# Expert weights in chunks of 2 MB, and gated rows added by products with diagonal matrices

## The chip, the cores and the metric

The kernel runs on one core of a Trainium2 chip. The core has TensorE (PE in the profile), VectorE (DVE), ScalarE (ACT), GpSimd (POOL) and a queue engine, SyncE (SP), beside 16 DMA engines that all queues share. The metric is the device time of one execution in microseconds (us), lower is better.

## What is computed

One layer: a token mixer, cross-attention, and a mixture of experts, then a last RMSNorm. There are 512 tokens of 1024 channels, all in f32. The change lies in the mixture of experts and in what follows it:

```python
logits = ht @ w_router + b_router
top_val, top_idx = lax.top_k(logits, 4)          # 4 of 32 experts for each token
gate = softmax(top_val)
# for each expert e and its tokens xb:
hc  = xb @ w1[e] + b1[e]                         # w1[e]: 1024 x 2048, 8 MB
glu, lin = min(hc[:, :1024], 7), clip(hc[:, 1024:], -7, 7)
act = glu * sigmoid(1.702 * glu) * (lin + 1)
y   = act @ w2[e] + b2[e]                        # w2[e]: 1024 x 1024, 4 MB
out[token] += gate * y                           # over the token's four experts
return rmsnorm(x + out, g_final)
```

All 32 experts are used, so 32 x 12 MB of expert weights are read from HBM.

## The kernel before

Each engine has a program written out by hand, in the order in which its instructions stand; semaphores order the engines among each other. A dense part comes first (token mixer, cross-attention, router), up to about 710 us. Then the experts run one by one.

**Chunks and ring.** An expert's weights come as 12 chunks of 1 MB: 8 of layer one (`W1`), a row of 2048 numbers (8 KB) in each of 128 partitions, and 4 of layer two (`W2`), two rows of 1024 beside each other in a partition, 8 KB too. `EC` is 12. The ring has `SLOTS` = 15 places: 12 in the tile `ring` and 3 in `moe`, the last of which lies over the f32 biases. SP issues all loads (`load`, L485). For the first 15 it waits until the dense part has freed the memory (L488 to L497): two go at 596 us, two until 617, two at 665, and nine at 710. From then on `refill` loads chunk k when PE has used chunk k - 15, which PE tells by `w_used`, once a chunk. A chunk has landed when all its 16 DMA engines have reported to `w_ring` of its place.

**PE.** For each expert `up` (L1902) adds into PSUM, chunk by chunk: for each chunk, group j of 32 tokens (an expert takes 3, 3 or 2 groups in turn) and quarter s of the columns, one product of 128 x 32 by 128 x 512. Four of them with different s run beside each other in the array. An f32 product shows as two records. `down` (L1926) does the same with layer two and 256 columns. The order is up(p), turns of small tiles, down(p-1). `x_turn` (L1860) transposes an expert's tokens, and a set of 32 products at L1979 makes the first expert's. The last expert's layer two is `last_down` (L1952), whose result stays on the chip (`y_last`).

**The end.** Results of experts go to HBM (`y_main`, the last but one expert's to `y_late`). POOL gathers them by token with indirect DMAs, 512 KB each: 16 `early_row` (L656), u = 4t + k for token tile t and choice k, into eight places `y_rows`, and four `late_row` (L661). The first waits until the last chunk of down(30) has landed. In DVE's `add_row` (L1510) and `add_late` (L1516) each is multiplied by its gate and added to `res`. PE's `last_rows` (L1970) makes the last expert's share, four token tiles of two 64-row products each, and DVE's `add_last` (L1544) adds it. ACT sums squares (L1037), then DVE and ACT make the norm (L1549, L1551, L1040, L1555) and SP stores the tile (L539). POOL, DVE and PE first read `n_over`, a count of experts with more tokens than fit; the trace shows no such work.

**The last chunk** is loaded in two pieces (L524), 8 partitions with a semaphore of their own (`w_edge`) and 120 partitions.

## Time and profile before

| | us |
|---|---|
| median of 3 runs | 1824.0 |
| lowest, highest | 1822.47, 1825.4 |
| the profiled execution | 1821.48 |
| its span in the profile | 1819.8 |

The mean granted clock of TensorE in it was 0.987 of full speed. Busy in the span: PE 1700.5 us, DVE 459.2, ACT 385.8, POOL 101.3. The 16 DMA engines moved 505.72 MB, a mean of 278 GB/s.

A profile is of one execution. "DMA share" is the mean busy share of the 16 DMA engines; packets whose times overlap make it a little more than 1. Windows give a stretch in us from the span's start. A row in order of time has its start, its length, the engine and line, the operation, and in square brackets the idle time ahead of it with what ended it. SPq is the instruction queue of SP, and its DMA_DIRECT2D rows are issues, not transfers.

### The profile page before, as it was taken

What the parts mean: (1) busy time and instruction counts of PE and PEld (TensorE: products, weight loads), DVE (VectorE), ACT (ScalarE), POOL (GpSimd) and SP (SyncE); (2) the same over time, 40 slices, a digit from 0 to 9 for tenths busy, and PEclk for the clock granted to TensorE, in tenths of its full rate; (3) what the DMA queues carried; (4) which work ended last, traced back from release to release, by engine and by line L of the source; (5) the groups of instructions that cost most, each with busy time, mean ns of one, the idle gap of its engine ahead of it and who ended that gap; (6) DMA issues with size and microseconds to landing.
All of it is one profiled execution on the core that took longest, in us unless ns stands there. A gap on an engine that the chain in (4) does not pass through costs nothing.

```text
span 1819.8 us, 36146 instructions
## 1 busy us (share of the span) xinstructions
PE 1700.5 (93%) x15618; PEld 943.4 (52%) x15618; DVE 459.2 (25%) x846; ACT 385.8 (21%) x602; POOL 101.3 (6%) x185
## 2 busy tenths in 40 slices
PE   7999999999999997999999999999999999999982
PEld 5766687788788766434343434333343343343330
DVE  4354426324544345700010101010000000000007
ACT  5464233324334325001000000000000010000001
POOL 0010000000000020000000000000000000000012
PEclk9999999999999999999999999999999999999996
DMA  7202221224225333999999999999999999999996
GB/s 237 70 24 82 82 101 50 70 93 162 93 84 194 116 93 148 363 392 376 410 399 407 402 407 401 403 410 398 410 404 402 411 404 402 411 401 409 409 333 256
DMA packets 105718, 505.72 MB, mean 278 GB/s; under 512 B 10519, under 2 KB 21287, under 8 KB 56327
## 3 DMA queue, kind: packets, MB, share of 16 engines
q1 hardware_dynamic: 83911, 461.40, 64.5%
q0 software_dynamic: 8352, 29.01, 5.1%
q10 hardware_dynamic: 13312, 13.12, 2.1%
q8 instruction: 125, 2.05, 0.5%
q14 instruction: 18, 0.15, 0.0%
HBM read 488.28 MB, written 15.20 MB: 277 GB/s over the span
## 4 chain that ended last, share of the span: by engine, by line
PE 59%; SPq 18%; DMA 13%; DVE 4%; issue 2%; ACT 2%; POOL 1%; ACTq 0%; DVEq 0%
SPq L485 18%; PE ps L1902 16%; PE ps L1582 9%; PE ps L1583 9%; PE ps L1584 9%; PE ps L1926 7%; DMA ring<-in_w_exp_in 5%; DMA ring<-in_w_exp_out 5%; DMA moe<-in_w_exp_in 2%; PE ps L1679 1%; PE ps L1734 1%; PE ps L1753 1%; DVE work L1510 1%; DMA work<-y_main,work 1%; PE ps L467 1%
## 5 line engine op out<-in xcount | busy, mean ns | idle before, releaser
L1902 PE MATMUL ps<-ring,moe 128*32 128x512 f32 x4408 | 490.2, 594 | 24.0 <-DMA ring<-in_w_exp_in 23.6
L1902 PEld LDWEIGHTS ps<-ring,moe 128*32 128x32 f32 x4408 | 131.2, 110 | 366.2 <-issue 270.4
L1477 DVE TENSOR_SCALAR moe<-ps 128x768 f32<-128x768 f32 (+1 forms) x32 | 28.0, 875 | 883.6 <-PE ps L1902 883.6
L1926 PE MATMUL ps<-ring,moe 128*32 128x256 f32 x4320 | 240.4, 379 | 7.4 <-DMA ring<-in_w_exp_out 7.4
L1051 DVE TENSOR_TENSOR wl<-raw,wh 128x1024 fp32r<-128x1024 f32 x104 | 126.3, 1224 | 259.4 <-ACT wh L712 259.4
L1926 PEld LDWEIGHTS ps<-ring,moe 128*32 128x32 f32 x4320 | 129.3, 110 | 108.5 <-DMA ring<-in_w_exp_out 12.6
L712 ACT ACTIVATE wh<-raw 128x1024 fp32r<-128x1024 f32 x104 | 108.9, 1057 | 255.8 <-PE ps L1584 255.2
L1582 PE MATMUL ps<-oph,wh 128*128 128x512 f32 x384 | 151.5, 394 | 2.4 <-DVE work L1184 1.6
L952 ACT ACTIVATE moe<-ps 128x768 f32<-128x768 f32 (+1 forms) x32 | 23.8, 744 | 596.5 <-DVE moe L1477 596.5
L1583 PE MATMUL ps<-opl,wh 128*128 128x512 f32 x384 | 150.2, 391 | 0.0
L1584 PE MATMUL ps<-oph,wl 128*128 128x512 f32 x384 | 150.1, 391 | 0.0
L1902 PE MATMUL ps<-moe 128*32 128x512 f32 x1096 | 124.4, 594 | 7.4 <-DMA moe<-in_w_exp_in 7.3
L1582 PE MATMUL ps<-wh,oph 128*128 128x512 f32 x288 | 113.8, 395 | 3.8 <-DVE opl L1222 3.0
L1583 PE MATMUL ps<-wl,oph 128*128 128x512 f32 x288 | 112.2, 389 | 0.0
L1584 PE MATMUL ps<-wh,opl 128*128 128x512 f32 x288 | 112.1, 389 | 0.0
L1582 PEld LDWEIGHTS ps<-oph,wh 128*128 128x128 f32 x384 | 72.8, 190 | 19.4 <-issue 3.6
L1902 PEld LDWEIGHTS ps<-moe 128*32 128x32 f32 x1096 | 32.4, 110 | 93.2 <-issue 64.7
L1584 PEld LDWEIGHTS ps<-oph,wl 128*128 128x128 f32 x384 | 72.5, 189 | 15.5
L1583 PEld LDWEIGHTS ps<-opl,wh 128*128 128x128 f32 x384 | 72.6, 189 | 14.5
L612 POOL CAST sel_c<-work 96x32 bf16 (+1 forms) x64 | 16.8, 288 | 933.8 <-DVE moe L1331 905.3
L1582 PEld LDWEIGHTS ps<-wh,oph 128*128 128x128 f32 x288 | 54.1, 188 | 17.4 <-issue 4.7
L1584 PEld LDWEIGHTS ps<-wh,opl 128*128 128x128 f32 x288 | 54.1, 188 | 11.5
(298 smaller groups left out, 1520.1 us busy)
## 6 DMA issues: line engine op xcount, KB each, us to landing
ring<-in_w_exp_in SPq DMA_DIRECT2D x205, 1024.0 KB, 28.6
ring<-in_w_exp_out SPq DMA_DIRECT2D x103, 1024.0 KB, 28.8
moe<-in_w_exp_in SPq DMA_DIRECT2D x51, 1024.0 KB, 29.1
raw<-in_w_in SPq DMA_DIRECT2D x26, 1024.0 KB, 5.2
moe<-in_w_exp_out SPq DMA_DIRECT2D x24, 1024.0 KB, 28.3
raw<-in_w_ckv SPq DMA_DIRECT2D x8, 1024.0 KB, 5.1
y_main<-moe ACTq DMA_DIRECT2D x84, 96.0 KB, 9.3
raw<-in_w_ret_o SPq DMA_DIRECT2D x4, 1024.0 KB, 5.1
```

What stands on the lines that cost most here:

```text
L467: ins = nc.tensor.matmul(ps[:, 6 + dt, :], v_x[:, m, a:a + P], prob_t[:, hd % 2, m * T:(m + 1) * T], start=(m == 0), stop=(m == MT - 1))
L485: sp.dma_start(held(s), expert_chunk(e, c)).then_inc(w_ring[s], 16)
L712: nc.scalar.activation(wh[:, slot, :], raw[:, c % RAW, g % 2 * PC:(g % 2 + 1) * PC], ACT.Copy).then_inc(w_hi, 1)
L952: nc.scalar.activation(glu_s[:, 0:g], ps[:, 0:g, 0:256].rearrange("p j (n a) -> p j a n", a=2), ACT.Silu, scale=ALPHA).then_inc(s_ready, 1)
L1051: nc.vector.tensor_tensor(wl[:, slot, :], raw[:, g // 2 % RAW, g % 2 * PC:(g % 2 + 1) * PC], wh[:, slot, :], ALU.subtract).then_inc(w_lo, 1)
L1477: nc.vector.tensor_scalar(act_n[:, 0:g], ps[:, 0:g, 256:512].rearrange("p j (n a) -> p j a n", a=2), 1.0 - LIMIT, 1.0 + LIMIT, ALU.max, AL ...
L1510: nc.vector.scalar_tensor_tensor(res[:, t, :], y_rows[u % ROWS], gate[:, t, k:k + 1], res[:, t, :], ALU.mult, ALU.add).then_inc(row_used, 1)
L1582: nc.tensor.matmul(o, a_hi_, b_hi_, start=start, stop=False)
L1583: nc.tensor.matmul(o, a_hi_, b_lo_, start=False, stop=False)
L1584: return nc.tensor.matmul(o, a_lo_, b_hi_, start=False, stop=stop)
L1902: ins = nc.tensor.matmul(ps[32 * s:32 * s + 32, j, :], xt[:, k, 32 * j:32 * j + 32], w[:, s, :, :], start=False, stop=(k == KT - 1), tile_ ...
L1926: ins = nc.tensor.matmul(y_bank(s, j), at[:, a, j, q, :], w[:, a, s, :], start=False, stop=(q == W2 - 1 and a == 1), tile_position=(0, 32 ...
```

## The change

Chunks become 2 MB: a partition holds two rows of layer one or four of layer two, 16 KB in one piece of HBM. `W1` is 4, `W2` 2, `EC` 6. The ring has 7 places, six in `ring` and one, number 5 (`EDGE`), in `moe`; `w_used` counts once for 2 MB. SP fills three places before the dense part ends and four after it.

As partition p of chunk c now holds rows 2p and 2p+1 of its 256 rows, the tokens' transposes take every other channel (`by_pair`). For layer two a partition holds rows 4p to 4p+3, so `up` takes the columns of each product in pairs: two numbers, then two left out. The products stay the same in number and size.

The last chunk is loaded in eight pieces of 2, 4, 6, 8, 10, 12, 14 and 72 partitions.

At the end DVE first makes eight matrices of 128 x 128, a gate on the diagonal (`gate_d`, in memory of the router). PE multiplies with them the four late gathers and the four early ones of the last token tile, and adds them in PSUM to the last expert's share. DVE's `add_row` 12 to 15 and all `add_late` are gone. The late gathers have other places in memory.

```diff
-W1 = KT
-W2 = KT // 2
+W1 = KT // 2
+W2 = KT // 4
 EC = W1 + W2
-SLOTS = EC + 3
+EH = 2 * CH
+SLOTS = EC + 1
...
-        ring = sb("ring", [P, EC, CH])
+        ring = sb("ring", [P, EC, EH])
...
         def held(s):
-            return ring[:, s, :] if s < EC else m_(5120 + CH * (s - EC), CH)
+            return m_(5120, EH) if s == EDGE else ring[:, s if s < EDGE else s - 1, :]
...
-        late = ring[:, 9:11, :].rearrange("p c (b n) -> p (c b) n", b=2)
+        late = [m_(6144, D), m_(9216, D), m_(10240, D), w_(4096, D)]
...
             if c < W1:
-                return w_exp_in[0, bass.ds(e, 1), c * P:(c + 1) * P, :].rearrange("o p n -> p (o n)")
+                return w_exp_in[0, bass.ds(e, 1), 2 * P * c:2 * P * c + 2 * P, :].rearrange("o (p a) n -> p (o a n)", a=2)
             q = c - W1
-            return w_exp_out[0, bass.ds(e, 1), 2 * P * q:2 * P * q + 2 * P, :].rearrange("o (p a) n -> p (o a n)", a=2)
+            return w_exp_out[0, bass.ds(e, 1), 4 * P * q:4 * P * q + 4 * P, :].rearrange("o (p a) n -> p (o a n)", a=4)
...
-                elif 2 <= s < 6:
-                    sp.wait_ge(w_lo, 2 * (DENSE - RAW + s - 1))
-                elif s == 6:
+                elif 1 <= s < 3:
+                    sp.wait_ge(w_lo, 2 * (DENSE - RAW + 2 * s))
+                elif s == 3:
                     sp.wait_ge(w_used, DP)
-                elif s == EC + 1:
+                elif s == EDGE:
...
-            for rows, landed in ((slice(0, 8), w_edge), (slice(8, P), w_ring[(CHUNKS - 1) % SLOTS])):
+            row = 0
+            for n, landed in zip((2, 4, 6, 8, 10, 12, 14), w_edge):
+                rows = slice(row, row + n)
                 sp.dma_start(held((CHUNKS - 1) % SLOTS)[rows, :], expert_chunk(final, EC - 1)[rows, :]).then_inc(landed, 16)
+                row += n
...
-            def add_late(t):
-                dve.wait_ge(late_in[t], 16)
-                dve.wait_ge(row_used, 4 * t + 4)
-                nc.vector.scalar_tensor_tensor(res[:, t, :], late[:, t, :], names["glate"][:, t:t + 1], res[:, t, :],
-                                               ALU.mult, ALU.add).then_inc(late_used, 1)
+            def diagonal(n, column):
+                nc.vector.tensor_scalar(gate_d[n], ident, column, None, ALU.mult).then_inc(diag_ready, 1)
...
+            def by_pair(rows, k):
+                return rows.rearrange("p (c n a) -> p c a n", c=W1, a=2)[:, k // 2, k % 2, :]
...
-                for k in range(KT):
-                    w = chunk_in(None if over is not None else up_chunk(n, k), over, k).rearrange("p (g s n) -> p s g n", g=2, s=4)
-                    for j in range(g):
-                        for s in range(4):
-                            ins = nc.tensor.matmul(ps[32 * s:32 * s + 32, j, :], xt[:, k, 32 * j:32 * j + 32], w[:, s, :, :],
+                for c in range(W1):
+                    w = chunk_in(None if over is not None else up_chunk(n, c), over, c).rearrange(
+                        "p (a g u n l v) -> p a u l g n v", a=2, g=2, u=2, l=2, v=2)
+                    for a in range(2):
+                        k = 2 * c + a
+                        for j in range(g):
+                            for s in range(4):
+                                ins = nc.tensor.matmul(ps[32 * s:32 * s + 32, j, :], xt[:, k, 32 * j:32 * j + 32], w[:, a, s // 2, s % 2, :, :, :],
...
+            def gated_rows(t, n, rows, stop=False):
+                for h in range(2):
+                    ins = nc.tensor.matmul(ps[:, 2 * t + h, :], gate_d[n], rows[:, 512 * h:512 * h + 512],
+                                           start=False, stop=stop, skip_group_check=True)
+                return ins
+
             def last_rows():
                 pe.wait_ge(gl_kept, 1)
                 pe.wait_ge(y_kept, NE)
                 for t in range(TT):
+                    own_rows(t)
+                pe.wait_ge(diag_ready, TT + TOPK)
+                for t in range(TT - 1):
+                    pe.wait_ge(late_in[t], 16)
+                    gated_rows(t, t, late[t], stop=True).then_inc(last_done, 1)
+                for k in range(TOPK):
+                    u = (TT - 1) * TOPK + k
+                    pe.wait_ge(row_in[u % ROWS], 16 * (u // ROWS + 1))
+                    gated_rows(TT - 1, TT + k, y_rows[u % ROWS])
+                pe.wait_ge(late_in[TT - 1], 16)
+                gated_rows(TT - 1, TT - 1, late[TT - 1], stop=True).then_inc(last_done, 1)
```

SP's queue at the end of the weights, before: the last whole chunk, the two pieces of the last one, and the load of `n_over` that follows.

```order
L485 DMA ring<-in_w_exp_out 128x2048
L524 ISA [waits w_used]
L524 DMA ring<-in_w_exp_out 8x2048
L524 ISA
L524 DMA ring<-in_w_exp_out 120x2048
L527 TENSOR_LOAD work [waits route_done]
```

And now (rows that only count registers left out):

```order
L489 DMA ring<-in_w_exp_out 128x4096
L535 ISA [waits w_used]
L535 DMA ring<-in_w_exp_out 2x4096
...
L535 DMA ring<-in_w_exp_out 4x4096
...
L535 DMA ring<-in_w_exp_out 6x4096
...
L535 DMA ring<-in_w_exp_out 8x4096
...
L535 DMA ring<-in_w_exp_out 10x4096
...
L535 DMA ring<-in_w_exp_out 12x4096
...
L535 DMA ring<-in_w_exp_out 14x4096
...
L538 DMA ring<-in_w_exp_out 72x4096
L541 TENSOR_LOAD work [waits route_done]
```

Two issues of the last chunk have become eight; nothing else has come between.

PE's queue from the last chunk on, before; the last two rows are `last_rows`.

```order
L1952 MATMUL ps<-ring,moe 32x512 [waits w_ring8,w_edge]
L1952 MATMUL ps<-ring,moe 32x512 x7
L2013 TENSOR_LOAD work [waits route_done]
...
L2016 UNCONDITIONAL_BRANCH [waits y_kept]
...
L1970 MATMUL ps<-moe 128x512 [waits y_kept,gl_kept]
L1970 MATMUL ps<-moe 128x512 x7
```

And now:

```order
L1967 MATMUL ps<-ring,moe 32x512 [waits w_edge4,w_edge5,w_edge3,w_edge6,w_edge2,w_ring2,w_edge1,w_edge0]
L1967 MATMUL ps<-ring,moe 32x512 x15
L2046 TENSOR_LOAD work [waits route_done]
...
L2049 UNCONDITIONAL_BRANCH [waits y_kept]
...
L1982 MATMUL ps<-moe 128x512 [waits y_kept,gl_kept]
L1982 MATMUL ps<-moe 128x512 x7
L1987 MATMUL ps<-moe,work 128x512 [waits late_in0,diag_ready]
...
L1987 MATMUL ps<-moe,work 128x512 [waits late_in1]
...
L1987 MATMUL ps<-moe,work 128x512 [waits late_in2]
...
L1987 MATMUL ps<-work 128x512 [waits row_in4]
...
L1987 MATMUL ps<-work 128x512 [waits row_in5]
...
L1987 MATMUL ps<-work 128x512 [waits late_in3]
```

Behind the last expert's share stand sixteen full products with the diagonal matrices, each pair behind the gather that it needs; the rows of the other gathers are left out.

DVE's queue at the very end, before, from the norm of the first tile on.

```order
L1551 RECIPROCAL small<-small 128x1 [waits dve_chain]
L1510 SCALAR_TENSOR_TENSOR work<-work 128x1024 [waits row_in4]
L1555 SCALAR_TENSOR_TENSOR work<-work,small 128x1024 [waits n_sqrt]
...
L1510 SCALAR_TENSOR_TENSOR work<-work 128x1024 [waits row_used,row_in5]
...
L1510 SCALAR_TENSOR_TENSOR work<-moe,work 128x1024 [waits row_used,row_in6]
...
L1516 SCALAR_TENSOR_TENSOR work<-ring,work 128x1024 [waits row_used,late_in3]
L1544 TENSOR_TENSOR work<-ps,work 128x1024 [waits late_used,last_done]
L1549 TENSOR_SCALAR small<-small 128x1 [waits n_sq]
...
L1555 SCALAR_TENSOR_TENSOR work<-work,small 128x1024 [waits n_sqrt]
```

And now:

```order
L1564 RECIPROCAL small<-small 128x1 [waits dve_chain]
L1568 SCALAR_TENSOR_TENSOR work<-work,small 128x1024 [waits n_sqrt]
L1562 TENSOR_SCALAR small<-small 128x1 [waits n_sq]
...
L1568 SCALAR_TENSOR_TENSOR work<-work,small 128x1024 [waits n_sqrt]
L1557 TENSOR_TENSOR work<-ps,work 128x1024 [waits last_done]
L1562 TENSOR_SCALAR small<-small 128x1 [waits n_sq]
...
L1568 SCALAR_TENSOR_TENSOR work<-work,small 128x1024 [waits n_sqrt]
```

The four `add_row` and the `add_late` of the last tile are gone from between the norms, so the last `add_last` stands right behind the third norm, with only PE to wait for.

## Rows read from the trace of the kernel before

**Rows 1.** The page, part 2: DMA engines, busy tenths in 40 slices of the span.

```profile
DMA  7202221224225333999999999999999999999996
```

**Rows 2.** Busy time by stretch (start:end us, length, engines, PEclk, DMA share, GB/s).

```profile
core 0: us, PE busy (x) PEld busy (x) DVE busy (x) ACT busy (x) POOL busy (x), PEclk, DMA share, GB/s
740.00:800.00 60.00, 58.06 (x652) 21.86 (x648) 29.90 (x83) 5.52 (x8) 2.78 (x6) 0.97 0.94 358
1200.00:1300.00 100.00, 94.41 (x1172) 36.84 (x1168) 6.95 (x12) 8.67 (x14) 4.44 (x9) 1.00 1.02 406
1750.00:1765.00 15.00, 12.52 (x200) 6.14 (x196) 1.38 (x2) 1.09 (x2) 0.74 (x1) 1.00 0.69 220
```

**Rows 3.** PE in order of time, a wait for a chunk (start, length).

```profile
1149.91 1.92 PE L1902 MATMUL ps<-ring,moe 128*32 128x512 f32 x16 [0.91 <-DMA ring<-in_w_exp_in]
```

**Rows 4.** The page, part 6: a DMA issue, KB each, median us to landing.

```profile
ring<-in_w_exp_in SPq DMA_DIRECT2D x205, 1024.0 KB, 28.6
```

**Rows 5.** DMA queues from 800 to 1700 us: packets, MB, share of 16 engines.

```profile
q1 hardware_dynamic: 46975, 342.09, 94.0%
...
q10 hardware_dynamic: 11520, 9.97, 3.2%
```

**Rows 6.** The same for 1412 to 1430 us, in which only weights move.

```profile
q1 hardware_dynamic: 1035, 7.54, 101.2%
```

**Rows 7.** The chain that ended last, three experts (start, length, what).

```profile
922.68 20.60 PE ps L1902 x192
...
956.56 13.74 PE ps L1902 x128
...
1014.14 20.60 PE ps L1902 x192
```

**Rows 8.** SP queue in order of time: the loads that fill the ring.

```profile
664.94 47.86 SPq L485 DMA_DIRECT2D ring<-in_w_exp_in  x8
712.84 1.47 SPq L485 DMA_DIRECT2D moe<-in_w_exp_in  x3
738.68 0.33 SPq L485 DMA_DIRECT2D ring<-in_w_exp_in  x1
741.25 8.05 SPq L485 DMA_DIRECT2D ring<-in_w_exp_out  x4
```

**Rows 9.** PE in order of time, the first two experts.

```profile
735.86 20.77 PE L1902 MATMUL ps<-ring,moe 128*32 128x512 f32 x192
...
761.81 11.48 PE L1902 MATMUL ps<-ring,moe 128*32 128x512 f32 x96
```

**Rows 10.** The end, all engines in order of time.

```profile
1764.26 0.99 POOL L656 DMA_INDIRECT work<-y_main,work  x1 [40.85 <-DMA ring<-in_w_exp_out]
...
1779.75 2.48 PE L1952 MATMUL ps<-ring,moe 128*32 128x512 f32 x16 [3.75 <-DMA ring<-in_w_exp_out]
...
1787.01 5.78 PE L1970 MATMUL ps<-moe 64*128 64x512 f32 x16 [4.79 <-issue]
...
1795.42 0.93 POOL L661 DMA_INDIRECT ring<-y_late,work  x1 [0.30 <-issue]
...
1810.91 1.28 DVE L1516 SCALAR_TENSOR_TENSOR work<-ring,work 128x1024 f32<-128x1024 f32 x1
1812.30 1.23 DVE L1544 TENSOR_TENSOR work<-ps,work 128x1024 f32<-128x1024 f32 x1
...
1815.37 1.28 DVE L1555 SCALAR_TENSOR_TENSOR work<-work,small 128x1024 f32<-128x1024 f32 x1 [0.27 <-ACT small L1040]
```

**Rows 11.** DMA issues of the whole run: the gathers of late rows.

```profile
ring<-y_late,work POOLq DMA_INDIRECT x4, 7.7
```

**Rows 12.** The chain that ended last: eight records, four full f32 products.

```profile
658.37 3.71 PE ps L467 x8
```

**Rows 13.** Busy time by stretch at the end, columns as in rows 2.

```profile
1785.00:1790.00 5.00, 2.99 (x8) 1.56 (x10) 4.79 (x4) 0.00 (x0) 3.84 (x4) 0.50 0.97 357
1790.00:1795.00 5.00, 2.79 (x10) 0.84 (x8) 4.69 (x5) 0.00 (x0) 4.03 (x4) 0.88 1.01 359
```

More of the change, by code:

```diff
@@ L518, in _ @@
                         refill(some[i], W1 + q, down_chunk(1 + i, q), m * (TURN * EC))
-            final = expert_at(NE - 1)
+            *some, final = [expert_at(NE - 3 + i) for i in range(3)]
+            for i in range(2):
+                for c in range(W1):
+                    refill((some[1], final)[i], c, up_chunk(NE - 2 + i, c))
+                for q in range(W2):
+                    refill(some[i], W1 + q, down_chunk(NE - 3 + i, q))
             for q in range(W2 - 1):
@@ L534, in _ @@
                         for c in range(EC):
-                            load(b % NE, c, c)
+                            load(b % NE, c, c if c < EDGE else c + 1)
             for tt in range(TT):
@@ L1962, in gates_turn, with own_rows @@
                 ins.then_inc(gl_made, 1)
+            def own_rows(t):
+                for h in range(2):
+                    rows = slice(64 * h, 64 * h + 64)
+                    nc.tensor.matmul(ps[:, 2 * t + h, :], gate_l[rows, t * P:(t + 1) * P], y_last[rows, :],
+                                     start=True, stop=False, skip_group_check=True)
+            def gated_rows(t, n, rows, stop=False):
+                for h in range(2):
+                    ins = nc.tensor.matmul(ps[:, 2 * t + h, :], gate_d[n], rows[:, 512 * h:512 * h + 512],
+                                           start=False, stop=stop, skip_group_check=True)
+                return ins
             def last_rows():
```

71 lines of the change are left out of this document (35 added, 36 removed).

## The prediction

> **What bounds the kernel now.** I read the page's slices first, then windows, queues and the order of time at both ends. From about 720 us to 1765 us the DMA engines are full [rows 1], and in the middle of the expert phase their share is 1.02 while PE is busy 94% of the time [rows 2]: PE works off a chunk of 16 records in 1.92 us and then waits 0.9 us for the next one [rows 3]. The arithmetic agrees. In 900 us the weight queue moves 342.09 MB [rows 5], so an expert of 12.58 MB takes 12.58 / 342.09 x 900 = 33.1 us. PE, when it had chunks in stock, made three experts between 922.68 and 1014.14, 30.5 us each [rows 7]. So the transfer of the weights is the bound, by 2.6 us an expert. A chunk lands 28.6 us after its issue [rows 4], though one is issued every 33.1 / 12 = 2.8 us: some ten are on their way at once, and no wait of SP is on the path.
>
> Two stretches are different. Between 740 and 800 us the DMA share is only 0.94 [rows 2]: there the ring is full of landed chunks and SP waits for PE. And between 1750 and 1765 us, with chunks still missing, the share is 0.69 at 220 GB/s [rows 2]: some of the 16 engines have finished their part of the last chunks and others have not. The last chunk starts PE at 1779.75 [rows 10]. Behind it DVE is the bound: of the end at 1816.65 the last steps are the late row of the last tile at 1810.91, the last addition at 1812.30, and the norm [rows 10].
>
> **Packets of 16 KB.** A packet has a part that does not depend on its size. Weights alone: 1035 packets and 7.54 MB take 101.2% of 16 engines for 18 us, 291.5 us of engine time [rows 6]. ACT's stores have small packets: 11520 and 9.97 MB take 3.2% of 16 x 900 us, 460.8 us [rows 5]. Two equations, a for a packet and b for a MB: 1035a + 7.54b = 291.5 and 11520a + 9.97b = 460.8 give a = 7.4 ns and b = 37.6 us. With the weight row of rows 5 for the other one a is 6.5 ns, and the rounding of 3.2% is worth 0.7 ns: 5.8 to 8.1 ns. A chunk counts 144 packets (46975 for 342.09 MB [rows 5]: 128 of data, and 16 which report). Six of the 384 chunks are loaded in the dense part; for the other 378 half of 54,432 packets go. The gain is 27,216 x 7.4 ns / 16 = 12.6 us (9.9 to 13.8). No row here has a weight packet of 16 KB, so nothing shows that a piece of that size travels whole and without a price of its own; the lower bound is no gain, and below it a loss of the same size. I take 12.6, since the rows from 1 KB to 8 KB lie on one line. An expert then takes 32.7 us, and PE's 30.5 still hide behind that.
>
> The Trainium skill's page "DMA: Bandwidth & Descriptors", in the section on the anatomy of one DMA, gives a transfer 2.0 us of fixed cost beside its bytes. For 189 transfers fewer that would be an estimate of 378 us, if they stood one behind the other. Rows 4 speak against it here: the cost lies beside some ten other transfers. I leave 2% to it.
>
> **Places of 2 MB.** The ring falls from 15 MB to 14, and SP gets a place back only when PE has used 2 MB. Just before PE's even MB the queue is 1 + 1 = 2 MB behind where it was. This costs only while the ring is what limits, 740 to 800 us. The fill after the dense part is nine chunks in one go at 710 to 714 us [rows 8] and becomes eight; the first refills, at 738.68 and 741.25 [rows 8], become one at 741.2. PE's first expert takes 20.77 us for 8 MB and the second starts at 761.81 [rows 9]; the first refill of the second comes when 2 MB are used, 5.2 us later, instead of 2.6. At the 0.38 to 0.42 MB/us of the stream 2 MB are 4.8 to 5.3 us, and a little is lost on top while it catches up: I take +5.5. Bounds: 1 MB, 2.6, and 3 MB, 8. After 800 us PE gains on the DMA and the places are plentiful: beside the 2 MB in PE's hands 12 MB are on their way or landed, 33 us of stream against the 28.6 us that a chunk needs in the queue.
>
> **Strided operands.** `up` now reads two numbers and skips two, and the transposes take every second channel. No row of before has a product of this kind. They are the same products; if they ran slower, the 2.2 us an expert between 30.5 and 32.7 are the cover. `up` is (20.60 + 13.74 + 20.60) / 3 = 18.3 us of an expert [rows 7], so the cover is gone from 12% on. I take nothing.
>
> The Trainium skill's "SBUF — State Buffer", in its section on the DMA port swizzle, states that a read runs at full bandwidth with at least two hits in each line of 16 bytes. Two f32 out of four are just two hits. By it this edit costs nothing, and no run here shows it.
>
> **The last chunk.** Eight issues stand where two stood, but issued some 30 us ahead of need, like the ones before them [rows 4]; their time at SP is hidden, and SP has nothing behind them but the outputs. The split moves rows between DMA engines, towards those that a small piece uses. Whether these are the ones that are early, rows 2 do not say. A whole engine's share of 2 MB is 8 packets of 16 KB, 8 x 0.62 = 5 us; that is the most it can gain, if the late engines get none. If a late one gets more than its share I give it 3 us. Between them I take 0. One more term: from the landing of the chunk that lets POOL go (1764.26) to the last one (1779.75) 4 MB take 15.5 us [rows 10], where at 0.42 MB/us they would take 10; the row gathers take the rest, packet by packet. With half as many weight packets among them I take 1.5 us off.
>
> So PE gets its last chunk 12.6 - 5.5 + 1.5 = 8.6 us earlier, at 1771.2 (without the start of the stream moved, since the loads at 710 us hang on the dense part alone).
>
> **The tail.** Before, from 1779.75: 2.48 us of work, 4.8 us until `last_rows` start at 1787.01, 5.78 us of them, and DVE behind [rows 10]. Now the chunk is 32 records, 3.8 us [rows 3] to 5.0; I take 4.4. Then 4.8, and 5.8 for the last expert's share. Then 16 full f32 products: four take 3.71 us [rows 12], one 0.93, together 14.8. Then the last `add_last` and the norm, 1812.30 to 1816.65, 4.35 us, and 0.1 to hand over. The end is 1771.2 + 4.4 + 4.8 + 5.8 + 14.8 + 4.5 = 1805.5, against 1816.65: -11.2. Two other ways must be shorter. The gathers: the last one was issued at 1795.42 and takes 7.7 us [rows 10, 11], 1803.1; now 7.1 earlier, 1796.0; two products and the norm behind it end at 1802.4. DVE: sixteen row additions and four late ones become twelve, it saves 8 x 1.28 [rows 10] = 10.2 us of a chain that was full, and ends its first three tiles before PE is ready with the last. The eight diagonals are small and stand where DVE waits for the first gather. So PE takes DVE's place as the bound, and most of what DVE saves goes into the 14.8 us of PE.
>
> **Sum.** On the profiled execution's 1821.5 us: -12.6 + 5.5 - 1.5 - 2.6 = -11.2, 1810.3. The median of the runs is 2.5 us above it, so I forecast 1824.0 - 11.2 = 1813. Its own range, from the bounds of packet, ring and last chunk: 1805 to 1820.
>
> **Rivals.**
> (1) The 16 KB packets are no cheaper, say because they travel in pieces. Then 12.6 us are missing: 1825, no change. For it: no row has such packets. Against it: the law holds over a factor of eight.
> (2) PE is cold at the end. It stands idle before `last_rows`, and the granted clock there is 0.50, then 0.88 after some us of work [rows 13]. At 1.2 GHz the 16 products take twice 14.8 us: 1828, slower. It decides from about 12 of the 16 products in the low clock. Against it: PE now works without a stop, and the clock rose during the 5.78 us before.
> (3) Strided reads hold PE up. From 12% on in `up` PE is the bound; at twice the time an expert takes 30.5 + 18.3 = 48.8 us, 16 more than 32.7, for 31 experts 500 us: some 2310 us, far slower.
> (4) The coarse ring lets DMA queues run dry later on too, because a chunk must land on all engines, the late ones too, before its place comes back. At 1 us an expert 1839. Against it: 33 us of stock.
> (5) Better than the sum: the split spares the late engines (5 us), or the ring costs only its 1 MB (3 us): 1803.
>
> **Chances.** The forecast 0.60; (1) 0.11; (2) 0.07; (3) 0.07; (4) 0.05; (5) with the 2% above 0.10. A measurement of this kernel tells 0.2% from no change, 3.6 us. Faster is the forecast and (5), 0.70; within 0.2% is (1) and a little of the forecast's upper end, 0.13; slower is (2), (3), (4) and the loss below (1), 0.17. The range takes in (1), (2) and most of (5): 1803 to 1829, leaving out (3), (4) and the rest of (5).
>
> **What would show it.** Right: half as many packets in the weight queue, and less than 33.1 us an expert in mid phase, with MB in 900 us up by 1.2% to about 346; a lower DMA share than 0.94 in 740 to 800; `up` at 20.6 us where PE has stock; the last chunk at about 1771; PE busy without a gap to the last product, at about 1801, and DVE waiting for it. Wrong: a weight queue with as many packets or the same MB in 900 us; a longer `up`; a PE clock of 0.5 in the last products; DVE or a gather named as what the last addition waits for.

## The result, and the profile after

The changed kernel takes 1837.7 us (median of 6 runs, 1833.8 to 1841.6). The kernel before took 1824.9 (6 runs beside it, 1822.5 to 1825.8). The ratio is 1.0074, interval 1.0061 to 1.0088: 13.5 us slower (12.8 by the medians), where 11 us less were forecast. Two of the four runs of experiment 8 below came out in a slower state (2141.4 and 2149.5 us) and are left out. The profiled execution took 1835.6 us with a span of 1833.9, against 1821.5 and 1819.8.

Busy time by stretch of the changed kernel (start:end us, length, busy us of PE, PEld, DVE, ACT, POOL with counts, PEclk, DMA share, GB/s), as rows 2:

```profile
740.00:800.00 60.00, 58.48 (x625) 23.65 (x616) 31.49 (x93) 4.06 (x6) 3.82 (x7) 0.97 0.87 321
800.00:900.00 100.00, 100.00 (x1229) 43.69 (x1231) 6.95 (x12) 9.57 (x17) 4.47 (x9) 1.00 1.00 379
1750.00:1765.00 15.00, 10.96 (x104) 3.28 (x96) 3.08 (x10) 1.09 (x2) 0.00 (x0) 1.00 0.98 294
1765.00:1780.00 15.00, 11.53 (x153) 5.75 (x153) 0.00 (x0) 0.00 (x0) 3.79 (x4) 0.77 0.74 200
1780.00:1800.00 20.00, 13.99 (x97) 4.90 (x99) 3.25 (x3) 1.47 (x3) 5.55 (x6) 0.75 0.94 237
```

Two stretches went wrong. From 740 to 900 us the stream is slower than before: 321 GB/s to 800 us, where rows 2 had 358. And at the end the rate falls to 294, 200 and 237 GB/s, and stays there to 1800 us. In the first and third of these stretches the DMA engines are nonetheless busy (0.98, 0.94): the packets themselves take longer. Between them, from 1765 to 1780 us, a part of the engines is idle as well (0.74).

The DMA queues from 800 to 1700 us (packets, MB, share of 16 engines), as rows 5:

```profile
q1 hardware_dynamic: 23575, 343.35, 93.7%
q0 software_dynamic: 2736, 9.44, 3.3%
q10 hardware_dynamic: 11520, 9.97, 3.2%
```

Half the packets, as forecast, for 343.35 MB instead of 342.09: 0.4% more, not 1.2%.

The chain that ended last, three experts (start, length, what), as rows 7:

```profile
900.68 21.74 PE ps L1916 x183
922.42 1.13 PE ps L1871 x8
...
956.52 10.36 PE ps L1940 x192
...
968.25 14.47 PE ps L1916 x118
...
996.36 21.74 PE ps L1916 x183
```

A three-group `up` (L1916) takes 21.74 us instead of 20.60, a two-group one 14.47 instead of 13.74, the transposes of `x_turn` (L1871) 1.13. Three experts, 900.68 to 996.36, take 95.7 us where they took 91.5. `down` (L1940, 10.36) has its time of before: its operands are read as before.

PE in order of time at the end, as rows 10:

```profile
1791.29 3.61 PE L1967 MATMUL ps<-ring,moe 128*32 128x512 f32 x32
1797.05 5.25 PE L1967 MATMUL ps<-ring,moe 128*32 128x512 f32 x32 [2.15 <-DMA ring<-in_w_exp_out]
1806.86 5.40 PE L1982 MATMUL ps<-moe 64*128 64x512 f32 x16 [4.57 <-issue]
1812.43 5.39 PE L1987 MATMUL ps<-moe,work 128*128 128x512 f32 x12 [0.16 <-DMA moe<-y_late,work]
...
1824.52 1.88 PE L1987 MATMUL ps<-work 128*128 128x512 f32 x4
```

The last chunk starts PE at 1797.05. Before that was at 1779.75, and 1771.2 was forecast. From there on the forecast holds nearly: 5.25 us for the chunk (4.4 forecast), 4.57 idle (4.8), 5.40 for `last_rows` (5.8), then PE almost without a gap through the products with diagonal matrices. The way from the last chunk to the end (1830.8) is 33.7 us; 36.9 before, 34.3 by the terms of the forecast.

The last chunk isn't alone in being late. The chain that ended last goes through the row gathers, of which these are two pieces (start, length, what):

```profile
1777.77 21.53 DMA work<-y_main,work
...
1804.53 7.76 DMA moe<-y_late,work
```

One gather of 512 KB takes 21.53 us from its issue to its landing. The first late row lands at 1812.29, when PE is just through with the last expert's share (1812.26). So the way through the late chunk and the way through the slow gathers are equally long.

So of 14.1 us of span, 17.3 arise before the last chunk starts PE, and 3.2 come back in the tail. The experiments take the 17.3 apart.

### The profile page after: what moved, and what is told of

Its sections match the earlier page's. It is cut to its first block, busy times and chain, and to the rows that moved or that the text cites. A ratio compares the mean times of both kernels' runs of the same rounds, so it can differ in the third digit from the quotient of the medians.

```text
span 1833.9 us, 35462 instructions
## 1 busy us (share of the span) xinstructions
PE 1757.5 (96%) x15650; PEld 998.6 (54%) x15650; DVE 451.4 (25%) x846; ACT 386.0 (21%) x602; POOL 101.5 (6%) x185
## 4 chain that ended last, share of the span: by engine, by line
PE 79%; DMA 15%; DVE 3%; ACT 2%; issue 1%; SPq 0%; POOL 0%; ACTq 0%; POOLq 0%; DVEq 0%
PE ps L1916 28%; PE ps L1940 12%; DMA ring<-in_w_exp_in 10%; PE ps L1590 9%; PE ps L1591 9%; PE ps L1592 9%; DMA ring<-in_w_exp_out 2%; PE ps L1871 1%; PE ps L1687 1%; DMA work<-y_main,work 1%; PE ps L1742 1%; PE ps L1761 1%; PE ps L1904 1%; PE ps L1880 1%; PE ps L471 1%; PE ps L1987 1%
## 5 line engine op out<-in xcount | busy, mean ns | idle before, releaser
L1916 PE MATMUL ps<-ring,moe 128*32 128x512 f32 x4688 | 542.2, 616 | 8.6 <-DMA ring<-in_w_exp_in 8.2
L1916 PEld LDWEIGHTS ps<-ring,moe 128*32 128x32 f32 x4688 | 166.8, 108 | 365.8 <-issue 335.3
L1940 PE MATMUL ps<-ring,moe 128*32 128x256 f32 x4704 | 266.5, 383 | 9.8 <-DMA ring<-in_w_exp_out 6.2
L1940 PEld LDWEIGHTS ps<-ring,moe 128*32 128x32 f32 x4704 | 143.6, 111 | 121.7 <-issue 9.7
L1916 PE MATMUL ps<-moe 128*32 128x512 f32 x816 | 96.4, 615 | 0.9 <-DMA moe<-in_w_exp_in 0.9
L1916 PEld LDWEIGHTS ps<-moe 128*32 128x32 f32 x816 | 30.5, 108 | 61.5 <-issue 58.1
```

The costliest lines, as they stand in the source:

```text
L1916: ins = nc.tensor.matmul(ps[32 * s:32 * s + 32, j, :], xt[:, k, 32 * j:32 * j + 32], w[:, a, s // 2, s % 2, :, :, :], start=False, stop=(k ...
L1940: ins = nc.tensor.matmul(y_bank(s, j), at[:, a % 2, j, 2 * q + a // 2, :], w[:, a, s, :], start=False, stop=(q == W2 - 1 and a == 3), tile ...
```

## Experiments

Times are compared with the kernel before run on the same chip beside each: its medians were 1825.6, 1825.0 and 1823.2 us for the three groups of four kernels (experiments 1 to 4, 5 to 8, 9 to 12). Where two experiments are compared, differences of medians are given, and of the ratios where they say something else. One ratio is known to about 2 us, a difference of two to some 3 us. "Best" is the kernel of experiment 5.

**1. The last chunk in one transfer** (changed kernel):

```
-            for n, landed in zip((2, 4, 6, 8, 10, 12, 14), w_edge):
-                rows = slice(row, row + n)
-                sp.dma_start(held((CHUNKS - 1) % SLOTS)[rows, :], expert_chunk(final, EC - 1)[rows, :]).then_inc(landed, 16)
...
+            load(final, EC - 1, (CHUNKS - 1) % SLOTS)
```

> The changed kernel, but the last weight chunk comes in one transfer of 128 partitions instead of eight transfers of 2 to 72 partitions. Theory A: transfers of a few partitions put the 16 DMA engines in each other's way, so that the whole stream runs at about half rate (200 to 237 GB/s between 1765 and 1800 us, packets of 16 KB at 1.0 to 1.2 us instead of 0.62) while they are in flight; without them the rate stays near 400 GB/s up to the last packet, the last chunk starts PE some 8 to 12 us earlier than 1797, and the time is about 1827 (1824 to 1831). Rival B: the low rate at the end is that of the engines that are late anyhow (half the engines have finished), and the split spares the late ones; then the last chunk comes 0 to 5 us later and the time is 1838 to 1843.

Measured: 1821.0 us, ratio 0.9979 (0.9968 to 0.9990). The eight transfers alone cost the changed kernel 17 us (by the two intervals some 14 to 20): more than its whole loss. Its busy time by stretch, and PE at the end in order of time:

```profile
1750.00:1765.00 15.00, 13.67 (x120) 3.69 (x116) 0.00 (x0) 0.81 (x1) 0.00 (x0) 1.00 0.99 414
1765.00:1780.00 15.00, 13.31 (x201) 6.38 (x193) 3.09 (x10) 1.09 (x2) 5.58 (x6) 1.00 0.69 273
1780.00:1800.00 20.00, 16.09 (x100) 4.69 (x102) 15.12 (x12) 3.35 (x5) 10.39 (x11) 0.74 0.87 323
```

```profile
1787.51 9.23 PE L1958 MATMUL ps<-ring,moe 128*32 128x512 f32 x64
1798.51 3.70 PE L1973 MATMUL ps<-moe 64*128 64x512 f32 x16 [1.77 <-issue]
```

To 1765 us the stream runs at 414 GB/s, where the changed kernel had 294. The chunk is no longer waited for: PE runs through the last four MB, 64 records from 1787.51, in one piece. The gathers are faster too. From 1780 to 1795 us the row of their queue is, for the changed kernel and for this one:

```profile
q0 software_dynamic: 773, 2.82, 83.5%
```

```profile
q0 software_dynamic: 1346, 4.90, 86.1%
```

773 packets in 83.5% of 16 engines' 15 us are 0.26 us each, 1346 in 86.1% are 0.15. So the cut slowed the other queue's packets as well.

In this execution PE itself is what is late. Not by strided reads: `down` of expert 30, which reads as before, takes 17.7 us (1767.66 to 1785.4) where experiment 12 has 10.6. The last 24 of its 192 records alone take 6.8 us, with stops of 0.4 to 0.8 us between them, for which the profile names no cause. The changed kernel's trace and those of experiments 2 and 3 have such stops too, Best's and experiment 12's have none. The profiled execution took 1825.5 us and is the slowest of the ten, so a part of these stops isn't in the median of 1821.0.

The time is below the 1824 to 1831 of theory A, in its direction; rival B is out.

**2 to 4. The tail alone, the plain reads, and the cut of the kernel before.** Experiment 2 puts the diagonal matrices into the kernel before, as the changed kernel has them:

```
-            def add_late(t):
...
+            def diagonal(n, column):
+                nc.vector.tensor_scalar(gate_d[n], ident, column, None, ALU.mult).then_inc(diag_ready, 1)
...
-            add_row(12)
...
-            add_late(3)
```

Experiment 3 reads layer one with contiguous columns in the changed kernel (and so its biases, and the channels of the transposes; as many numbers are multiplied, but not the reference's):

```
-    "p (a g u n l v) -> p a u l g n v", a=2, g=2, u=2, l=2, v=2)
+    "p (a g s n) -> p a s g n", a=2, g=2, s=4)
```

Experiment 4 loads the last chunk of the kernel before in one transfer:

```
-            for rows, landed in ((slice(0, 8), w_edge), (slice(8, P), w_ring[(CHUNKS - 1) % SLOTS])):
-                sp.dma_start(held((CHUNKS - 1) % SLOTS)[rows, :], expert_chunk(final, EC - 1)[rows, :]).then_inc(landed, 16)
+            load(final, EC - 1, (CHUNKS - 1) % SLOTS)
```

> The kernel before with one part of the change alone: late rows and last tile by products with diagonal gate matrices; weights as before, in chunks of 1 MB. Theory: the way from the start of PE's last chunk to the end falls from 36.9 us to about 34, as it did in the changed kernel (33.7), and the time is 1822 (1820 to 1824). Rival: the f32 products at the end are in PE's low clock when the last chunk is smaller, or the tail of the changed kernel is only shorter since its last chunk comes so late that all row gathers are long done; then the tail is 36 to 42 us here and the time 1824 to 1830.

> The changed kernel with the operands of layer one read as contiguous columns and the transposes taking contiguous channels: the same number of products and bytes, but channels are paired with the wrong rows and columns of the weights, so layer one's numbers are not the reference's. Theory A: the strided f32 reads are what makes a group of `up` take 21.8 us instead of 20.6; with plain columns `up` is 20.6 again and x_turn 0.8, three experts take 91.5 us instead of 95.7, and the ring gives places back sooner between 740 and 900 us: of the 9 us lost there about 3 to 4 come back, time 1834 (1832 to 1836). Rival B: `up` is slow for another reason (the write of a packet of 16 KB into a partition that PE reads); then it stays at 21.8 us and the time at 1838. Rival C: `up` is fast again but the stream is the bound all the same and the time moves by less than 1 us.

> The kernel before, but its last chunk in one transfer of 128 partitions instead of 8 and 120. Theory A (transfers of fewer than 128 partitions slow the stream while they are in flight; before, 1751 to 1757 at about 230 GB/s): the last chunk comes 2 to 4 us earlier, time 1822 (1820 to 1823). Rival B (the split moves work from late to early engines and is worth its price): 1825 to 1830.

Measured: 1821.6 us for the tail alone (ratio 0.9977, 0.9966 to 0.9988); 1833.6 for plain columns (1.0039, 1.0027 to 1.0052), 4.1 under the changed kernel by the medians and 6 by the ratios; 1822.4 for the kernel before with its last chunk whole (0.9986, 0.9973 to 0.9998). In all three the first theory holds; in experiment 4 the interval just leaves out no change. In experiment 3 a three-group `up` takes 20.60 us and an `x_turn` 0.81.

What the cut of 8 and 120 does to a packet can be read from the weight queue in 1751 to 1757 us, before and in experiment 4:

```profile
q1 hardware_dynamic: 182, 1.26, 89.0%
```

```profile
q1 hardware_dynamic: 278, 1.99, 80.0%
```

With the cut 182 packets take 89.0% of 16 engines' 6 us, 0.47 us each; without it 278 take 80.0%, 0.28 us each.

**5. Both good edits on chunks of 1 MB**: the diagonal matrices and the last chunk whole, in the kernel before (the diffs of experiments 2 and 4 together).

> The kernel before (chunks of 1 MB) with the products with diagonal matrices and the last chunk in one transfer of 128 partitions. Each alone gave 4.0 and 3.2 us. Theory A: they act at different places (the arrival of the last chunk, the way behind it) and add up: time 1818 (1816.5 to 1820). Rival B: with the chunk earlier the row gathers are what is late at the end, and the second gain is lost: 1820 to 1823. Beside it the changed kernel with its last chunk whole (1821.0) says what chunks of 2 MB are worth by themselves: by A they cost 3 us, by B nothing.

Measured: 1814.1 us, ratio 0.9941 (0.9928 to 0.9955), 10.9 us under the kernel before and the fastest of all. That is more than the 7.2 us of the two alone, which neither theory gave. One reading is that each edit makes way for the other: with the products at the end the chain of row additions on DVE is no longer what is late [rows 10], so an earlier chunk, and earlier gathers, are worth their whole time. That is argued and not shown: in the traces of experiments 2 and 4 ACT stands idle for 20.43 and 17.74 us ahead of its work on the results of expert 30, in the end for something that the profile does not name, and PE, which follows, runs through the last four MB in one piece there too. The chain of work at the end of Best:

```profile
1767.53 11.65 DMA work<-y_main,work
...
1779.20 1.30 DVE work L1510
...
1784.53 7.64 DMA moe<-y_late,work
...
1792.30 13.99 PE ps L1965 x32
1806.31 1.24 DVE work L1544
...
1809.37 1.28 DVE work L1555
```

Here the last chunk isn't in the chain, and DVE only with one addition, which gives a gather its place. The row gathers are: the first late row lands at 1792.17 (7.64 us after its issue), and 14 us of products and the norm follow. PE waits only 0.87 us for that row, so the way through the last chunk is nearly as long. Against Best, the changed kernel with its last chunk whole is 7 us slower. So chunks of 2 MB, with the strided reads that they bring, are a loss.

**6. Two transfers of 1 MB for each chunk of 2 MB** (changed kernel, last chunk whole):

```
-                sp.dma_start(held(s), expert_chunk(e, c)).then_inc(w_ring[s], 16)
+                for h in range(2):
+                    sp.dma_start(held(s)[:, CH * h:CH * h + CH], expert_chunk(e, c)[:, CH * h:CH * h + CH]).then_inc(w_ring[s], 16)
...
-                    pe.wait_ge(w_ring[k % SLOTS], 16 * (k // SLOTS + 1))
+                    pe.wait_ge(w_ring[k % SLOTS], 32 * (k // SLOTS + 1))
```

> The changed kernel with its last chunk whole, and each 2 MB chunk loaded by two transfers of 1 MB, the first and the second half of every row: packets of 8 KB as before, places of the ring, strided reads and tail as changed. It takes the packet size alone away. Theory A: the packet's own share of 7.4 ns is real and hidden only in part behind PE, whose expert takes 31.9 us: where the stream is the bound (after 1350 us) it is worth 0.36 us an expert over some 13 experts, 5 us: time 1826 (1824 to 1833). Rival B: packets of 16 KB are no cheaper than two of 8 KB, or PE hides them wholly: the time stays at 1821.

Measured: 1822.9 us, ratio 0.9994 (0.9985 to 1.0003), against 0.9979 with whole packets. The difference, 1.9 us by the medians and 2.7 by the ratios, lies between the theories, and the intervals overlap: packets of 16 KB, together with half as many transfers, are worth 0 to 5 us here, and surely not 12.6.

**7. The last chunk in eight transfers of 128 partitions** (changed kernel; an eighth of the columns each):

```
-            for n, landed in zip((2, 4, 6, 8, 10, 12, 14), w_edge):
...
+            w = EH // 8
+            for n, landed in enumerate(w_edge + [w_ring[(CHUNKS - 1) % SLOTS]]):
+                sp.dma_start(held((CHUNKS - 1) % SLOTS)[:, w * n:w * n + w],
+                             expert_chunk(final, EC - 1)[:, w * n:w * n + w]).then_inc(landed, 16)
```

> The changed kernel with its last chunk in eight transfers, as there, but each of all 128 partitions and an eighth of the columns (packets of 2 KB), instead of 2 to 72 partitions. Theory A: what slows the stream is that a transfer covers only some of the partitions, so that the engines write through the same few ports of SBUF; with 128 partitions in each the time is that of the whole transfer, 1821 (1820 to 1824, some 1 us for 7/8 more packets and 7 more issues). Rival B: it is the number of transfers (eight completions, eight waits); then the time stays at 1836 to 1838.

Measured: 1825.2 us, ratio 0.9999 (0.9989 to 1.0009). Twelve of the 17 us are back with as many transfers and as many waits as in the changed kernel. The stream keeps its rate for the most part: in the three stretches of the end it moves 373, 303 and 363 GB/s, where the changed kernel moved 294, 200 and 237 and experiment 1 moved 414, 273 and 323. The last of them:

```profile
1780.00:1800.00 20.00, 7.09 (x34) 1.90 (x36) 13.01 (x11) 1.88 (x2) 15.84 (x12) 0.65 0.98 363
```

Eight transfers with their packets of 2 KB cost some 4 us, a little above what theory A gave (the two aren't taken apart); the partitions in each cost the rest.

**8 and 9. The same cut far from the end.** In 28 experts the first chunk of layer two comes in two transfers, of 64 and 64 partitions (experiment 8) or 8 and 120 (experiment 9):

```
+   for rows, landed in ((slice(0, 64), w_mid[i]), (slice(64, P), w_ring[k % SLOTS])):
+       sp.dma_start(held(k % SLOTS)[rows, :], expert_chunk(some[i], W1)[rows, :]).then_inc(landed, 16)
```

> The changed kernel with its last chunk whole, and in 28 of the 32 experts the first chunk of layer two in two transfers of 64 partitions each, on the same queue, instead of one of 128. It measures the price of a transfer of few partitions far from the end, where nothing else changes. Theory A: half of the partitions reach half of the ports, so each such chunk goes at half rate and takes some 5 us more: with 28 of them, up to 140 us, of which PE hides at most 1 us an expert: time 1920 to 1965, packets of 16 KB at twice 0.61 us while they are in flight. The Trainium skill's page "SBUF — State Buffer", section on the DMA port swizzle, says that partitions 0 to 63 cover only the 8 even ports; its rule would be seen here in this way. Rival B: only counts of partitions that 16 does not divide, which leave engines out, are dear (2 to 14, 72, 120); 64 is divisible, and the time stays at 1821 to 1825.

> The changed kernel with its last chunk whole, and in 28 experts the first chunk of layer two in transfers of 8 and 120 partitions instead of one of 128, as the kernel before cuts its last chunk. 64 + 64 at this place cost 300 us, 10.7 us a chunk. Theory A: only transfers that leave half of the ports out are dear; 120 partitions reach all of them, and the price is that of 8 partitions, under 1 us a chunk: 1825 to 1850. Rival B: any transfer which isn't of 128 partitions hands its rows to the engines in another order, so that several write through one port at a time; then the price is that of the kernel before, where this cut of 1 MB cost 3.2 us, for 2 MB 3 to 10 us a chunk: 1900 to 2100.

Measured: 2101.6 us (two runs, 2096.7 and 2106.4) and 2150.9 us (four runs, ratio 1.1772, 1.1737 to 1.1806). Against 1821.0 that is 281 and 330 us, for 28 chunks 10.0 and 11.8 us each. (The 10.7 us in the expectation of experiment 9 were worked out from a median of 2123.9.) Experiment 8, by stretch: a stretch with whole chunks, and one with a cut chunk in flight; below them the weight queue in the same two stretches.

```profile
1012.00:1020.00 8.00, 8.00 (x97) 3.36 (x90) 0.00 (x0) 1.47 (x3) 0.00 (x0) 1.00 1.00 423
1022.00:1040.00 18.00, 14.24 (x113) 4.32 (x108) 0.00 (x0) 0.00 (x0) 0.00 (x0) 0.91 1.02 230
```

```profile
q1 hardware_dynamic: 227, 3.33, 98.1%
```

```profile
q1 hardware_dynamic: 281, 3.88, 94.1%
```

The engines are full in both (1.00 and 1.02), but move 423 GB/s in the one and 230 in the other. By the queue's row 227 packets take 98.1% of 16 engines for 8 us, 0.55 us each with the small ones among them; later 281 take 94.1% for 18 us, 0.96 us each. Experiment 9:

```profile
1121.00:1147.00 26.00, 16.54 (x146) 4.91 (x138) 0.00 (x0) 1.68 (x3) 0.00 (x0) 0.87 1.02 225
1148.00:1154.00 6.00, 2.46 (x12) 0.58 (x16) 0.00 (x0) 0.00 (x0) 0.00 (x0) 0.55 1.02 405
```

225 GB/s for 26 us around a cut chunk, 405 behind it. The changed kernel's stream is much like this from 1755 to about 1805 us: 180 to 256 GB/s in steps of 5 us, though with a part of the engines idle in some. Theory A of experiment 9 (only transfers which leave half of the partitions out are dear) is refuted; a cut of 8 and 120 is at least as dear as one of 64 and 64. Both expectations were too small as well: 2 MB at half rate would be 5 us more, and the cut costs 10 to 12. The slow stretch takes in the chunks around it.

The Trainium skill's "DMA: Bandwidth & Descriptors", in its sections on a DMA's semaphore count and on the descriptor swizzle, says that a transfer of 128 partitions gives each engine rows of one SBUF port, and that other counts are dealt over the largest k up to 16 that divides them (8 engines for 8 rows, 15 for 120, 12 for the changed kernel's 72). The measured halving fits engines that then meet at the same ports; no row here shows a port, so that stays an inference. The Trainium skill's "SBUF — State Buffer", section on the DMA port swizzle, makes 64 partitions reach half of the ports, which gives the half rate of experiment 8 but not its length.

**10. The grain of the ring alone**, in Best: two chunks of 1 MB are asked for when both places of 14 are free.

```
-                sp.wait_ge(w_used, turn + (DP + k - SLOTS + 1))
+                sp.wait_ge(w_used, turn + (DP + (k | 1) - 13))
```

**11. The strided reads alone**, in Best (the biases too; the numbers of layer one are not the reference's):

```
-    w = chunk_in(...).rearrange("p (g s n) -> p s g n", g=2, s=4)
+    w = chunk_in(...).rearrange("p (g u n l v) -> p u l g n v", g=2, u=2, l=2, v=2)
...
-    xrows[:, k * P:(k + 1) * P]
+    xrows.rearrange("p (c n a) -> p c a n", c=KT // 2, a=2)[:, k // 2, k % 2, :]
```

**12. Chunks of 2 MB without strided reads**: the changed kernel with the diffs of experiments 1 and 3 (again not the reference's numbers).

> The best kernel so far (before, with diagonal products and the last chunk whole; chunks of 1 MB, 1814.1) with waits of the ring that make it as coarse as the changed kernel's: two chunks of 1 MB are asked for together, when both their places of 14 are free, the fifteenth place unused but at the start. Packets, reads and products as before. It takes the grain of the ring alone. Theory A: it costs what the prediction took for it, 5.5 us (the ring is what limits from 740 to 900 us): 1819.5 (1817 to 1822), DMA share in 740 to 800 us down from 0.93 to about 0.87. Rival B: a start that comes later is made good later, since PE has stock: 1814 to 1816.

> The same best kernel with chunks of 1 MB, but layer one's weights and biases read as two numbers of every four, and the channels taken by the transposes as every second one, as in the changed kernel; the numbers multiplied are not those of the reference in layer one. It takes the strided reads alone. Theory A: a group of `up` takes 21.8 us instead of 20.6 here too, three experts 95.7 instead of 91.5, and though the stream's 33.1 us an expert cover this in the middle, the time grows by about 4 us, as the changed kernel lost 4.1 with plain columns: 1818 (1816.5 to 1820); PE busy 100% from 800 to about 1350 us. Rival B: with places of 1 MB the ring covers it and nothing is lost: 1813 to 1815.5. Rival C: the reads are slow only beside packets of 16 KB; `up` stays at 20.6.

> The changed kernel with its last chunk whole and plain columns and channels in layer one (which numbers are multiplied there is not the reference's): chunks of 2 MB, ring of 14 MB, packets of 16 KB, no strided reads. It closes the square of reads and chunk sizes. Theory A: the three terms add up: against the best kernel +5.5 for the ring, -2.6 for the packets (two transfers of 1 MB gave 1822.9 against 1821.0), time 1817 (1815 to 1819). Rival B: without strided reads PE no longer hides the cheaper packets, and they give up to 12.6 us from 800 us on: 1808 to 1812.

Measured, with Best at 1814.1 us (0.9941): the grain 1819.6 (0.9986, 0.9975 to 0.9997), 5.5 us more by the medians and 8 by the ratios; the strided reads 1817.9 (0.9975, 0.9955 to 0.9995), 3.8 and 6 us; 2 MB with plain reads 1815.5 (0.9958, 0.9944 to 0.9973), 1.4 and 3 us, which the intervals do not tell from nothing. All three times are those of theory A. Best by stretch, then the first stretch of experiments 10 and 12, and three of 11:

```profile
740.00:800.00 60.00, 58.11 (x652) 21.87 (x648) 32.47 (x93) 4.71 (x7) 2.78 (x6) 0.97 0.93 355
800.00:900.00 100.00, 100.00 (x1272) 40.24 (x1268) 6.95 (x12) 9.76 (x16) 4.48 (x9) 1.00 1.01 396
900.00:1350.00 450.00, 438.92 (x5428) 171.80 (x5420) 32.87 (x56) 40.58 (x65) 20.64 (x42) 1.00 1.02 404
```

```profile
740.00:800.00 60.00, 58.06 (x652) 21.84 (x648) 29.69 (x82) 5.52 (x8) 2.78 (x6) 0.97 0.89 342
```

```profile
740.00:800.00 60.00, 58.06 (x652) 22.08 (x644) 32.85 (x94) 4.71 (x7) 3.80 (x7) 0.97 0.87 319
```

```profile
740.00:800.00 60.00, 58.38 (x632) 27.61 (x624) 32.11 (x93) 4.38 (x7) 2.78 (x6) 1.00 0.93 347
800.00:900.00 100.00, 100.00 (x1234) 43.58 (x1236) 6.95 (x12) 9.49 (x16) 4.47 (x9) 1.00 0.98 381
900.00:1350.00 450.00, 450.00 (x5400) 189.67 (x5393) 32.86 (x56) 40.10 (x65) 20.63 (x42) 1.00 1.02 405
```

Share and rate from 740 to 800 us fall from 0.93 and 355 GB/s to 0.89 and 342 with the coarse waits, and to 0.87 and 319 with places of 2 MB. With strided reads the loss comes from 800 to 900 us (381 GB/s instead of 396), and PE is busy all of the time up to 1350 us (450.00 of 450 us, where it was 438.92). The reason stands in the chain: a group of `up` and an `x_turn` of experiment 11, with packets of 8 KB, and of experiment 12, with packets of 16 KB:

```profile
900.36 21.74 PE ps L1900 x183
922.10 1.13 PE ps L1858 x8
```

```profile
895.36 20.60 PE ps L1910 x192
915.96 0.81 PE ps L1865 x8
```

21.74 us with strided reads and 8 KB, 20.60 with plain reads and 16 KB. It is the reads, not the packets. Whether it is that numbers are left out, or that the operand is walked in one more step, is not taken apart. Rival C of experiment 11 and rival B of experiment 3 are out. The weight queue from 900 to 1700 us, of experiment 12 and of Best:

```profile
q1 hardware_dynamic: 21129, 307.73, 93.9%
```

```profile
q1 hardware_dynamic: 41976, 305.67, 94.3%
```

With larger packets there are 307.73 MB instead of 305.67, 0.7%, where PE isn't what holds the stream up. That is 5.4 us over these 800 us, and would nearly make up for the coarse ring: hence, as I read it, the 1.4 to 3 us between this kernel and Best. The times of experiments 10 and 12, which differ in packets and transfers and hardly otherwise, say the same: 4.1 us by the medians, 5 by the ratios. But this is the largest of the differences. Experiments 1 and 6 have 306.80 and 306.16 MB in these 800 us, 0.2%, and from 1350 to 1700 us, where PE has gaps, 134.11 and 134.32 MB. Over all kernels but those of experiments 8 and 9, the ones with packets of 16 KB have 306.67 to 307.85 MB, those with 8 KB 305.31 to 306.16.

## Why the prediction was wrong, point by point

**The last chunk** is the step that failed. It was put at 0, between -5 and +3 us, as if the cut only moved rows between engines that are early and late. It cost 17 us (experiment 1), and the profile of before had the sign of it: rows 2 show 220 GB/s in 1750 to 1765 us, which I read as engines that had run out of work. Part of it was that: experiment 1 has a share of 0.69 and 273 GB/s in 1765 to 1780 us too. But part was the cut of 8 and 120, which the kernel before pays for as well: 3.2 us (experiment 4), and some 7 with the new tail (experiment 5 against 2). The price was inside a stretch that I quoted; what I left out was to ask what a packet takes there: 0.47 us of an engine with the cut, 0.28 without. The bound of 5 us was one engine's share of one chunk, but the cut slowed every packet in flight, those of the gathers too (0.26 us instead of 0.15; one gather took 21.53 us, where Best has 11.65).

**The strided operands** were put at nothing, since an expert of PE's had 2.2 us of cover against the stream. They made `up` 5.5% slower (20.60 to 21.74), well under the 12% from which the cover would be gone, and still cost 4 us (experiments 3 and 11). The cover isn't there in the first stretch: from 740 to 900 us the ring is full, SP waits for PE, and what PE loses there the stream loses. I used that argument for the ring and not for PE. With the loss, PE is busy without a gap to 1350 us. The Trainium skill's "SBUF — State Buffer", which I cited for it (section on the DMA port swizzle), has a read with two hits in each line of 16 bytes at full bandwidth. These f32 products don't bear that out: the trace has 21.74 against 20.60 us.

**Packets of 16 KB.** The forecast of half as many packets held. The gain was put at 12.6 us over all experts, 1.2% of the stream. It is at most 0.7% where the stream is free (experiment 12; between experiments 1 and 6 none is seen from 1350 to 1700 us), and 1.9 to 2.7 us in all in the changed kernel (experiment 6), where PE is the bound up to 1350 us. That the rows from 1 KB to 8 KB lie on one line was no support: they are two sizes of packet, and two points always do. Transfers cost next to nothing each, as I took it: twice as many of them cost those 1.9 to 2.7 us, and not the 378 us of the estimate (the Trainium skill's "DMA: Bandwidth & Descriptors", in the section on the anatomy of one DMA, has its 2.0 us for transfers that GpSimd issues; SP issues the weights).

**Places of 2 MB** were put at 5.5 us. In experiment 12 the core moves 319 GB/s from 740 to 800 us instead of 355, 2.2 MB less or some 5.5 us of stream, and from 800 us on no less than Best. Experiment 10 gives 5.5 us by its medians and 8 by the ratios. By its first stretch it would be 2 us (355 to 342 GB/s); where the rest of it goes no single stretch shows. The term was of the right size, and its place is shown for places of 2 MB.

**The tail** was put at -2.6 us, with PE in DVE's place. It measured -3.2 between the two traces and -4.0 alone (experiment 2). Rival (2), the cold clock, didn't come: the products take 14.0 to 14.2 us in the traces (1792.30 to 1806.3 in experiment 5), a little less than the 14.8 worked out from rows 12. As forecast, PE is what DVE's last addition waits for.

**The sum.** With what was measured, from the kernel before: last chunk +17 against its own cut's 7 once the tail is in, +10; grain +5.5; reads +4; packets -2; tail -4. That is +13.5, against 13.5 measured. Most of this agreement is no check: the tail, the cut's 7, the 7 from Best to experiment 1 and the 17 are steps that lead from the one kernel to the other. What can be checked is that grain, reads and packets, each taken alone, give 7.5 us where the step from Best to experiment 1 is 7. By the ratios they would be 8, 6 and -3, together 11; each of them is known to some 3 us.

The range went to 1829 and the time is 1837.7, slower instead of faster: no rival held a price for the cut. Rival (3) had the right mechanism, but was priced only from where the cover of the steady phase ends: 500 us or nothing, where it is 4.

## What to carry to other kernels

Don't cut a transfer by partitions to have it land sooner while others are in flight; where it must be cut, cut it by columns with all 128 partitions in each (4 us for eight transfers here, against 17). A cover is a property of a stretch: before an edit is costed at nothing, look at every stretch in which the covering resource is itself held up by the edited one. And when a rate is low, look at what one packet takes before calling the engines idle.

## What was not expected of the hardware

- Two transfers of 64 and 64, or 8 and 120, partitions for one chunk of 2 MB bring the whole stream of the core from 423 or 405 to 225 to 230 GB/s for 18 to 26 us, 10.0 to 11.8 us lost each time, with the DMA share at 1.02.
- With an f32 moving operand of 128 x 512 that takes two numbers and skips two, a group of `up` is 5.5% slower (21.74 us against 20.60), and the transposes with every second channel 40% (1.13 us for eight against 0.81).
- PE's granted clock falls from its upper level (2.4 GHz, a share of 1.00) when PE idles for lack of chunks: a mean of 0.87 in the 26 us of experiment 9, 0.75 from 1780 to 1800 us in the changed kernel. The work behind such a wait takes longer: the 32 records of the last chunk take 3.64 us at a clock of 1.00 (experiment 12), 5.25 in the changed kernel behind 2.15 us of idle time (0.67), 6.53 in experiment 7 behind 10.85 us (0.54).
- What remains open: why a cut chunk disturbs the stream for four times its own share of it; what PE's stops and ACT's long waits in some of the traces near the end (experiments 1 to 4) wait for; and why the row gathers of the end, in Best the next thing that is late, take 11.65 and 7.64 us.
